# Streaming-encoder step: the sample stage's loads and products reordered, the last four MLP units taken tile by tile

## The reference, cut to what matters

```python
pr, pm, last = _project(x, shift, w_in, mu_shift)          # one input projection
o_rw, s_fin = _rwkv7(pr, state, ...)                        # 8 heads x 64, recurrence
qn, qr = _mla_q(pm, ...)                                    # latent attention: queries
c, kr = _mla_latent(pm, ...)                                # new latent and rotary key rows
o_at = softmax((qn.kn + qr.kr) * SCALE) v                   # kn, v are expanded from c (old and new rows)
mix = concat(o_rw, rmsnorm(o_at)) @ w_out
h = layernorm(ALPHA * x + mix)
y = layernorm(ALPHA * h + square(relu(h @ w_up)) @ w_down)  # 1024 -> 4096 -> 1024
```

## Time and profile before

| | |
|---|---|
| median of 3 runs | 2100.78 us (2094.28 to 2104.07) |
| the profiled execution's own time | 2088.48 us |
| its span, first to last instruction | 2086.7 us |
| mean granted TensorE clock | 0.947 of full speed |
| TensorE matmul busy | 1894.8 us (91%) |
| sample stage, from the barrier ahead to the barrier behind | 1017.4 to 1130.6 us |
| last stage | 1130.6 to 2086.7 us |

### The profile page before, as it was taken

The page is one execution under the profiler, slowest core; times in us unless marked ns, Lnnn a source line. Parts: engine busy times, 40 slices in busy tenths (PEclk is TensorE's granted clock), DMA queues, the critical chain, the costliest instruction groups (busy, mean ns, idle before and its releaser), DMA issues. The chain is left out here.

```text
span 2086.7 us, 39305 instructions
## 1 busy us (share of the span) xinstructions
PE 1894.8 (91%) x16543; PEld 1619.1 (78%) x16543; DVE 936.3 (45%) x1822; ACT 671.0 (32%) x1318; POOL 359.1 (17%) x333
## 2 busy tenths in 40 slices
PE   6999996788898889898697999999999999999995
PEld 6999983566666666665476788999999999999994
DVE  7610105445766665655425365333363333543335
ACT  2221211234344444444222113333333333333331
POOL 0000004232322221221200041301003110031000
PEclk9999996788999999999787999999999999999998
DMA  6352111101210110110504414444444444444441
GB/s 222 136 200 68 67 44 50 46 5 44 76 59 11 49 57 14 45 57 2 147 3 148 177 51 131 121 126 131 125 121 151 129 129 124 121 141 141 129 123 41
DMA packets 167890, 196.28 MB, mean 94 GB/s; under 512 B 18786, under 2 KB 142458, under 8 KB 166580
## 3 DMA queue, kind: packets, MB, share of 16 engines
q1 hardware_dynamic: 160692, 183.46, 28.3%
q0 software_dynamic: 2624, 9.50, 1.1%
q10 hardware_dynamic: 4432, 1.31, 0.3%
HBM read 165.82 MB, written 29.25 MB: 93 GB/s over the span
## 5 line engine op out<-in xcount | busy, mean ns | idle before, releaser
L664 DVE TENSOR_TENSOR c_wo_lo<-c_raw,c_wo_hi 128x1024 fp32r<-128x1024 f32 x96 | 117.6, 1225 | 465.8 <-ACT c_wo_hi L591 465.6
L803 PE MATMUL c_pY<-c_wo_hi,c_hl 128*128 128x512 f32 x576 | 226.1, 392 | 0.0
L803 PE MATMUL c_pY<-c_wo_lo,c_hh 128*128 128x512 f32 x576 | 225.8, 392 | 0.0
L803 PE MATMUL c_pY<-c_wo_hi,c_hh 128*128 128x512 f32 x576 | 225.3, 391 | 0.0
L591 ACT ACTIVATE c_wo_hi<-c_raw 128x1024 fp32r<-128x1024 f32 x96 | 101.8, 1061 | 332.1 <-PE c_pY L803 332.1
L547 POOL TENSOR_TENSOR c_hid<-c_relu 128x384 f32<-128x384 f32 x96 | 79.4, 828 | 677.2 <-ACT c_relu L606 677.2
L835 PE MATMUL c_pU<-c_zT_hi,c_wo_hi 128*128 128x384 f32 x768 | 151.2, 338 | 1.6 <-DVE c_zT_lo L659 1.6
L835 PE MATMUL c_pU<-c_zT_lo,c_wo_hi 128*128 128x384 f32 x768 | 148.6, 334 | 0.0
L835 PE MATMUL c_pU<-c_zT_hi,c_wo_lo 128*128 128x384 f32 x768 | 148.5, 334 | 0.0
L835 PEld LDWEIGHTS c_pU<-c_zT_hi,c_wo_hi 128*128 128x128 f32 x768 | 137.9, 188 | 9.7 <-DVE c_zT_lo L659 2.7
L835 PEld LDWEIGHTS c_pU<-c_zT_hi,c_wo_lo 128*128 128x128 f32 x768 | 134.5, 188 | 0.0
(11 more groups left out here) (455 smaller groups left out, 3419.1 us busy)
## 6 DMA issues: line engine op xcount, KB each, us to landing
c_raw<-w_down SPq DMA_DIRECT2D x96, 512.0 KB, 3.6
c_raw<-w_up SPq DMA_DIRECT2D x96, 512.0 KB, 4.8
scratch_p<-a_o SPq DMA_DIRECT2D x72, 154.0 KB, 1.8
a_w<-w_in SPq DMA_DIRECT2D x8, 1232.0 KB, 8.2
m_prev<-scratch_p SPq DMA_DIRECT2D x8, 896.0 KB, 4.6
m_pr<-scratch_p SPq DMA_DIRECT2D x5, 1232.0 KB, 5.4
b_pr<-scratch_p SPq DMA_DIRECT2D x4, 1232.0 KB, 5.4
scratch_h<-a_x POOLq DMA_DIRECT2D x9, 512.0 KB, 4.4
```

The lines of the kernel that those rows point to most:

```text
L664: dve.tensor_tensor(row_lo[U % 2], row_raw[U % 2][:, :], row_hi[U % 2].bitcast(F32), ALU.subtract).then_inc(S("row_lo"), 1)
L803: last = pe.matmul(pY[2 * t + half][:, :], x, w[:, 512 * half:512 * half + 512], start=first and a == 0, stop=final and a == 2, skip_group ...
```

## The change

In the sample stage (a) ScalarE issues no DMA any more; SyncE issues all loads, in the order masks, `wkT`, `latT`, `ropeT`, `state`, `lat`, and the eight small ones of `lat_new` behind them; (b) `absorb` is cut into its four banks, which stand between the steps of the squarings instead of ahead of `gram_q`; the scores of requests 0 and 1 come later; (c) both halves of `update` stand at the end of the requests, and VectorE does `variance` ahead of the last score.

In the last stage (d) the split of `w_out`'s block 7 stands ahead of that of tile 3 on ScalarE and VectorE; (e) in the last block TensorE forms the last four units' hidden columns one behind the other (with one `down` behind the first of them) and then adds all four units to tile 0, then to tile 1, then to tile 2; the rows and hidden columns of the last two units get slots of their own in a buffer that is free by then, so that four units are held at once; (f) VectorE finishes tile 0 alone and then tiles 1 and 2 with one `scales` for both; (g) SyncE issues the last three stores in place of GpSimd.

```diff
+        LATE = 4
+
+        spare_hi, spare_lo = (z[0][:, :, :].rearrange("p k n -> p (k n)") for z in (zT_hi, zT_lo))
+        row_hi, row_lo = (rows_ + [z[:, D * i:D * (i + 1)] for i in range(2)]
+                          for rows_, z in ((row_hi, spare_hi), (row_lo, spare_lo)))
+        hid_hi, hid_lo = ([h[:, :] for h in hid_] + [z[:, 2 * D + NT * i:2 * D + NT * (i + 1)] for i in range(2)]
+                          for hid_, z in ((hid_hi, spare_hi), (hid_lo, spare_lo)))
...
+        def slot_of(U):
+            return U % 2 if U < N_UNIT - 2 else 2 + U % 2
...
+            for t in range(BLK):
+                T = N_TILE - BLK + t
+                sp.wait_ge(S("y_last"), t + 1)
+                sp.dma_start(y_rows(T), of(T)).then_inc(S("y_last_stored"), 16)
+            sp.wait_ge(S("y_last_stored"), 16 * BLK)
...
-            for t in range(BLK):
-                T = N_TILE - BLK + t
-                pool.wait_ge(S("y_last"), t + 1)
-                pool.dma_start(y_rows(T), of(T)).then_inc(S("y_stored"), 16)
...
-                else:
+                elif slot_of(U) < 2:
                     act.wait_ge(S("row_used"), U - 1)
...
-                if U >= 2:
+                if U >= 2 and slot_of(U) < 2:
                     act.wait_ge(S("row_used"), U - 1)
...
+            out_high(7)
             turned_high(turned(3))
-            out_high(7)
...
+            out_low(7)
             turned_low(turned(3))
-            out_low(7)
...
+            T = N_TILE - BLK
+            add_residual(T, "y")
+            moments(T, "y")
+            scales(0, 1)
...
+            finish(T)
+            for t in (1, 2):
+                add_residual(T + t, "y")
+                moments(T + t, "y")
+            scales(1, 3)
+            finish(T + 1)
+            finish(T + 2)
...
-                with pe.Fori(1, NF // 2 - 1) as j:
+                with pe.Fori(1, NF // 2 - 1 - (b == N_BLK - 1)) as j:
...
+                    for U in range(e - LATE, e):
+                        pe.wait_ge(S("relu"), U - 1)
+                        up(b, U, U % 2)
+                        if U == e - LATE:
+                            down(U - 1, (U - 1) % 2)
+
+                    for t in range(BLK):
+                        for U in range(e - LATE, e):
+                            if t == 0:
+                                down_wait(U)
+                            last = down_part(t, slot_of(U), final=U == e - 1)
+                            if t == BLK - 1:
+                                last.then_inc(S("row_used"), 1)
...
     if engine == "tensor":
-        steps = plain("turn_latent", "turn_a", "queries", "turn_b", "gram_x", "turn_queries", "absorb", "gram_q")
-        steps += [("newton_t", 0)] + plain("own_z") + [("newton_x", 0)] + plain("own_y") + [("newton_t", 1), ("score", 0)]
-        steps += [("newton_x", 1), ("score", 1), ("newton_t", 2)] + plain("pick") + [("newton_x", 2), ("weights", 0)]
+        steps = plain("turn_latent", "turn_a", "queries", "turn_b", "gram_x", "turn_queries", "gram_q")
+        steps += [("newton_t", 0), ("absorb", 0), ("newton_x", 0)] + plain("own_z") + [("absorb", 1), ("newton_t", 1)]
+        steps += plain("own_y") + [("absorb", 2), ("newton_x", 1), ("absorb", 3), ("newton_t", 2), ("score", 0)]
+        steps += [("newton_x", 2), ("score", 1)] + plain("pick") + [("weights", 0)]
         steps += request(0, ["pick_turn"]) + request(1, ["scan_sa"]) + request(2, ["scan_y"])
-        steps += request(3) + [("update", 0)] + request(4) + [("update", 1)] + request(5)
-        return steps + [("weights", 7), ("context", 6), ("context", 7), ("values", None)]
+        steps += request(3) + request(4) + request(5) + [("update", 0)]
+        return steps + [("weights", 7), ("context", 6), ("context", 7), ("update", 1), ("values", None)]
     if engine == "vector":
...
-        steps += [("score", 4)] + plain("scan_y") + [("weights", 4), ("score", 5), ("weights", 5), ("update", 0)]
-        steps += plain("mean") + [("score", 6), ("weights", 6), ("update", 1), ("score", 7), ("weights", 7)]
-        return steps + plain("variance", "gate_out", "values")
...
+        steps += [("score", 4)] + plain("scan_y") + [("weights", 4), ("score", 5), ("weights", 5)] + plain("mean")
+        steps += [("score", 6), ("weights", 6)] + plain("variance") + [("score", 7), ("weights", 7), ("update", 0)]
+        return steps + plain("gate_out") + [("update", 1), ("values", None)]
+
+    steps = plain("turn_latent", "squares_8", "turn_a", "queries", "turn_b", "turn_queries")
+    steps += [("absorb", 0), ("newton_x", 0), ("absorb", 1), ("absorb", 2), ("newton_x", 1), ("absorb", 3), ("score", 0)]
+    steps += [("newton_x", 2), ("score", 1)] + plain("pick") + [("weights", 0)]
...
-            for b in range(B):
-                sp.dma_start(lat_new[:, b, :], c[T * b:T * b + T, :]).then_inc(S("latnew_landed"), 16)
+            sp.dma_start(ropeT[:, :, 0:PAST], io["cache_ropeT"].rearrange("b r n -> r b n")).then_inc(S("ropeT_landed"), 16)
+            for g in range(PAIRS):
+                sp.dma_start(state[:, g, :, :], io["state"][:, P * g:P * g + P, :].rearrange("b p v -> p b v"))\
+                  .then_inc(S("state_landed"), 16)
...
+            for b in range(B):
+                sp.dma_start(lat_new[:, b, :], c[T * b:T * b + T, :]).then_inc(S("latnew_landed"), 16)
...
         @block.scalar
         def _(act):
-            for g in range(PAIRS):
-                act.dma_start(state[:, g, :, :], io["state"][:, P * g:P * g + P, :].rearrange("b p v -> p b v"))\
-                   .then_inc(S("state_landed"), 16)
-            act.dma_start(ropeT[:, :, 0:PAST], io["cache_ropeT"].rearrange("b r n -> r b n")).then_inc(S("ropeT_landed"), 16)
```

More of the change, by code:

```diff
@@ L764, in _, with finish @@
                     hidden_low(U)
-            for t in range(BLK):
-                T = N_TILE - BLK + t
-                add_residual(T, "y")
-                moments(T, "y")
-                scales(t, t + 1)
-                x = of(T)
-                if t == 0:
-                    dve.wait_ge(S("ln2_g_landed"), 16)
-                    dve.wait_ge(S("ln2_b_landed"), 16)
+            def finish(T):
+                t, x = T % BLK, of(T)
                 step(dve.scalar_tensor_tensor(x, x, mean[:, t, 0:1], rows["ln2_g"][:, :], ALU.subtract, ALU.mult))
@@ L1943, in sample_steps @@
         steps += [("score", 2), ("weights", 2), ("score", 3), ("weights", 3)] + plain("scan_sa")
-        steps += [("score", 4)] + plain("scan_y") + [("weights", 4), ("score", 5), ("weights", 5), ("update", 0)]
-        steps += plain("mean") + [("score", 6), ("weights", 6), ("update", 1), ("score", 7), ("weights", 7)]
-        return steps + plain("variance", "gate_out", "values")
-    steps = plain("turn_latent", "squares_8", "turn_a", "queries", "turn_b", "turn_queries", "absorb")
-    steps += [("newton_x", 0), ("newton_x", 1), ("score", 0), ("score", 1)] + plain("pick") + [("newton_x", 2), ("weights", 0)]
+        steps += [("score", 4)] + plain("scan_y") + [("weights", 4), ("score", 5), ("weights", 5)] + plain("mean")
@@ L2078, in _ @@
                 if step == "absorb":
+                    k, g = divmod(v, 2)
                     pe.wait_ge(S("wkT_landed"), 16)
[L2081 to L2089 removed]
+                    pe.wait_ge(S("qnope_out"), g + 1)
+                    bank = J.fill(pe, ("abs", k, g))
+                    for hh in range(4):
+                        h = 4 * g + hh
+                        last = pe.matmul(bank[:, P * hh:P * hh + P], wkT[:, h, P * k:P * k + P], qnopeT[:, h, :],
+                                         start=True, stop=True)
+                    J.filled(last)
                 if step in ("gram_x", "gram_q"):
```

52 lines of the change are left out of this document (18 added, 34 removed).

## The result

The changed kernel's median is 2064.52 us (2063.78 to 2070.00, 4 runs), against 2097.97 for the kernel before beside it (4 runs): ratio 0.9843, 95% interval 0.9812 to 0.9875. Two later series of it gave 2065.69 and 2066.45 (ratios 0.9857 and 0.9862), and the kernel before had medians of 2095.9 to 2099.2 in five.

A forecast was written before the change was run, and what follows sets the result against it. TensorE, computing 1894.8 of 2086.7 us, bounds the kernel, so only its idle or half-clock time counts. Terms 10 + 2 + 0.5 + 2.9 + 8.7 + 0.3 = 24.4 us, off the median 2100.8, give 2076.4 us; range 2066 to 2089.

The forecast's parts named there:

- (a): Sample stage, ScalarE issuing no loads: `turn_queries` starts 10.3 us earlier, taken as a gain of 10 us.
- (b): Sample stage, `absorb` between squarings: 1.5 us of idle time and 0.5 us of clock, together 2 us, bounds 0 and 7.
- (c): Requests, updates last: `update` covers about half of TensorE's 1.14 us idle time, gain 0.5 us, bounds 0 and 1.1.
- (d): Last stage, block 7's split ahead of tile 3's: TensorE's wait of 2.94 us goes, gain 2.9 us.
- (g): End of the last stage, SyncE issuing the last stores: gain 0.3 us, bounds -0.5 and 1.
- the program waits for the loads: Sample stage: TensorE stands until 1041 to 1042 for its program; gain only 16.2 us, 2084.6 us; chance 0.20.
- (e, f): End of the last stage, four units by tiles: VectorE ends sooner after TensorE, gain 8.7 us, bounds 7.5 and 9.2.
- The tail: Last stage's end: keeps its length as units 30 and 31 wait the full 8.7 us; 2085.1 us; chance 0.05.
- the requests' clock: Requests: clock stays low until `values`, costing up to 37.6 us, so 2113.9 us; chance 0.10.
- Everything falls into place: Sample stage: `turn_queries` 3 us better, spread `absorb` 5 us more, `values` at full clock 3.5 more; 2064.9 us; chance 0.09.

The follow-up runs named there:

- e0_before: The kernel before run again with no edit, against the kernel before itself: median 2098.3 us (12 runs), ratio 1.001, interval 0.998-1.004.

## Why the forecast was right in its direction and too small

Like profiles averaged, the sample stage went from 111.1 us (three) to 96.7 (five with the changed kernel's instructions there), 14.4 us, and the last from 957.6 (four) to 942.2 (twelve), 15.4. That makes 29.8 of the 30 to 33.5 us; the forecast had 12.5 and 11.9. The sample stage is near the forecast in sum alone: undone one at a time its three parts cost 8.0, 9 to 10 and 5.5 us, which don't add, against 10, 2 and 0.5. In (b), (c) and (d) I had counted little or nothing for the clock. The rest of the miss against 2076.4 is that I subtracted from a median 3 us above the later ones, and what is left, up to 4 us, which lies in the scatter of the unchanged stages and stays open.

- **(a), 10 us.** The mechanism was right: ScalarE's first operation 0.8 us into the stage, TensorE's wait gone, `queries` 4.14 us. `turn_queries` started 10.0 us earlier in the first profile, and 13 us earlier in others, where `q_ready` decided. The rival that the program waits for the loads falls: in the first profile `turn_queries` started 16.7 us into the stage and the loads ran until 28. Its reason, the restart at the loads' end, was a coincidence (the packet had come 23.2 us into the stage, the loads ended at 25.1, and the block started at 25.7). What I didn't count: 10 us at this point are not 10 us at the stage's end. It gave 6 us alone and 8 as the last part; in the profiles the clock came up at another time.
- **(b), 2 us.** This is the step of the sample stage that failed: "I count 0.5 us" for the clock. The two runs without it lost 9 to 10 us. The bound of 7 had the mechanism, an earlier rise of the clock; I took a low value because the clock had been low although TensorE was "busy for 28.84 us". The mean of 0.69 over that stretch hid what happened in it: low until 39.5 us into the stage, up, and low again from 46.4 to 53.2, behind the gap of 2.32 us that I priced at its own length alone. The "issue" idle times themselves came to no gain.
- **(c), 0.5 us.** Here the sum failed too: undone it cost 5.5 us. The stretches show 1.28 us in the requests (38.76 to 37.48, above my bound of 1.1) and 3.15 us (6.94 to 3.79) because `values` runs at the full clock, which I had counted at nothing and given to a rival. The wait of 0.67 us ahead of it was in the trace.
- **(d), 2.9 us.** 3.2 us, and 2.8 to 2.9 more in three of the four profiles of the old last stage, in which the clock fell behind the wait. My profile was the fourth.
- **(e, f), 8.7 us.** 9.05 us, of which `scales` 2.2; the wait ahead of the third `up` was 0.2, not 0.4. **(g), 0.3 us:** 1.4, above its bound of 1.
- **Rivals.** The tail kept none of its length, the requests' clock was 1.00. "Everything falls into place" had the time (2064.9) and half of the reasons: `values` at the full clock, (b) above its upper bound. `turn_queries` came at 13 us into the stage in a part of the profiles alone.

## What to carry to other kernels

Price a short wait of TensorE by the clock behind it: a wait of 0.67 us went with a loss of 3.15 us by the low clock, one of 2.94 us with 2.9 in three of five profiles, and gaps of 0.4 to 1.6 us between small matmuls with a clock that stayed low for 14 us and more. It is a price with a chance, as a gap of 1.78 us in e0_before cost no clock; so give it a range. So place long products between groups of small ones, and put work that is ready ahead of a step that waits for another engine. Where the unchanged part varies by several microseconds, forecast from stages of several profiles of the kernel before, not from one.

## What the runs showed of the hardware

TensorE's program comes in blocks of 16 KB, here 127 matmuls with their weight loads. Where TensorE stood for one, its packet came 0.4 to 8.0 us after the first matmul of the block before (once 0.7 us ahead of it), and the first instruction 2.1 to 3.2 us behind the packet. In the sample stages of all seventeen profiles these packets came at least 3.3 us apart, whatever the semaphores allowed. One block can still pass faster: in e0_before the 127 matmuls from 278 on took 1.5 us, as the packet behind them had come 2.2 us ahead of them, while `absorb` ran. Runs of small matmuls longer than that wait. The Trainium skill, "Runtime: NRT & Kernel Launch", section "Instruction fetch mechanics", calls this cost mostly hidden; it is for most of this kernel, and not in this stage. The time of the clock's rise falls into few values (32, 36, 39, 46, 49, 53, 56, 63 us into the stage), and an execution with a late one costs more than many an edit is worth.
